# A decoder layer's expert lookup for three token tiles: row gathers replaced by two streamed tables and a gate matrix

## The chip, the cores and the metric

One of the eight cores of a Trainium2 chip runs the whole program. The metric is the device time of one execution in microseconds (us). All numbers are float32.

## The reference, cut to what matters

One layer over 512 prompt tokens (tiles 0 to 3 of 128 tokens) and 32 sample tokens (tile 4). First a mixing layer (input projection, gated MLP on chunks, windowed attention, output projection), then the expert layer below, then a final RMSNorm. The change is in the expert layer alone.

```
q = (xb @ w_q).reshape(TOK_BLK, PEER_HEADS, 2, DK_HALF)
s = jnp.einsum('thcd,hcnd->thcn', q, sub_keys).astype(jnp.float32)
s1, i1 = lax.top_k(s[:, :, 0], TOPK)
s2, i2 = lax.top_k(s[:, :, 1], TOPK)
...
eid = jnp.take_along_axis(cid, pos, axis=-1)
g = jax.nn.softmax(top_s, axis=-1).astype(xb.dtype)
hid = jax.nn.gelu(jnp.einsum('thkd,td->thk', u_tab[eid], xb), approximate=False)
return jnp.einsum('thk,thkd->td', g * hid, v_tab[eid])
```

With 8 heads and TOPK = 16 each token picks 128 of 16,384 experts. An expert is a row of 1,024 numbers in the table U and one in the table V (each table 67 MB). Its number is i1 * 128 + i2 of its two picks.

## The kernel before

Tensors lie with tokens or features on the 128 partitions. Each engine has its own instruction list and waits on semaphores; the order in each list is written out by hand. The stages in the order of TensorE's list:

- Tile 0 goes through projection, attention, output projection and its queries first. Its routing (the top-k chain on VectorE, `route(k)` for head k, cut into links that are dealt out between other work by `go_on`) gives expert numbers, and GpSimd begins to gather rows of U for it (`gather_u`).
- Tiles 1 to 4: projection (`project`), attention (`attend`), while VectorE takes the 128 dot products of tile 0 (`dots_to`).
- Output projection of tiles 1 to 4 (`project_out`), RMSNorm, `turn_xn` (the normalised tokens are transposed into `featT`), queries (`half_queries`, 416 columns each) and `key_scores`. Between these stand the V rows of tile 0: `gather_v` brings the 128 experts of one token as 128 rows (524 KB), and `weigh` multiplies them on TensorE with that token's weights. `weigh_first(4)` does four tokens, each in its own 32 columns of the array. The V ring has VR = 12 buffers.
- Tiles 1 to 3, then tile 4: the slot loop. Slot j of a tile is the j-th expert of each of its 128 tokens. `gather_both` brings 128 rows of U and V side by side (1.05 MB) into one of XR = 6 buffers; VectorE takes the dot product (`dot`); ScalarE makes gelu, times the gate, and a diagonal matrix of it (`weigh_slot`); TensorE multiplies that diagonal with the V rows and adds up in PSUM (`add_slot`, two matmuls of 512 columns). 20 slots of tile 1 are added by VectorE (`add_rows`). There are 3 x 128 slots for tiles 1 to 3 and 32 for tile 4, whose 32 tokens are spread over four groups of partitions. Routing of later tiles is dealt out between slots, and the last five of the eight query jobs (`JOBS`) stand between slots of tile 1.
- Each tile ends with `square_y`, `finish_y` and a store.

Of the kernel before, what the change touches and what calls it, by code (L numbers as in the profile page):

```python
# [10 lines left out]
AX = mybir.AxisListType  # L11
# [3 lines left out]
P = 128  # L15
# [32 lines left out]
NKEYS = 128  # L48
TOPK = 16
SLOTS = HEADS * TOPK  # L50
UR, VR, XR = 6, 12, 6
DG = 4
# [5 lines left out]
STEPS = [HEADS] * (NT - 1) + [HEADS // GROUPS]  # L58
FIRST = [sum(STEPS[:t]) for t in range(NT)]
NSTEP = sum(STEPS)  # L60

# [3 lines left out]
ROUTE_STEP = {g: [g + 2] for g in range(8, 24)} | {g: [2 * g - 22, 2 * g - 21] for g in range(24, 31)}  # L65
TOPS_ATT, EID_SAMPLE = 15, 5

JOBS_AHEAD = 3


def build(nc, x_p, x_s, k_cache, v_cache, gains, gain_cols, w_in, ln_gb, w_sT, b_sT, w_out, w_q, keysT, uv_tab,
# [3 lines left out]
    with ctx:  # L75
# [14 lines left out]
        def cut(area, a, *dims):  # L90
# [4 lines left out]
            if len(dims) == 3:  # L95
# [27 lines left out]
        x_ring = ([cut(area_r, s * 2 * D, 2 * D) for s in range(XR // 2)]  # L123
                  + [cut(area_r, 2 * PAIRS * TOK + s * 2 * D, 2 * D) for s in range(XR // 2)])
# [30 lines left out]
        y_junk = cut(area_v, NT * D, D)  # L155
# [17 lines left out]
        diag = [cut(area_c, s * P, P) for s in range(DG)]  # L173
# [3 lines left out]
        den = cut(area_v, (NT + 1) * D, NSTEP)  # L177
# [12 lines left out]
        tops = tops_all[:].rearrange("p (h k) -> p h k", h=HEADS)  # L190
# [28 lines left out]
        def wide(i, n):  # L219
            return bank[i].rearrange("p a b -> p (a b)")[:, 0:n]  # L220

        acc = bank[0]
        x_cur = wide(1, D)

# [31 lines left out]
        x_free, hid_ready, bent_ready, col_ready, diag_ready = (sem("x_free"), sem("hid_ready"), sem("bent_ready"),  # L256
                                                                sem("col_ready"), sem("diag_ready"))
        head_exped, head_gated, summed_den = sem("head_exped"), sem("head_gated"), sem("summed_den")
        eye_ready, numbered = sem("eye_ready"), sem("numbered")
        x_added, rest_added = sem("x_added"), sem("rest_added")  # L260
# [3 lines left out]
        samp_gates = sem("samp_gates")  # L264
# [78 lines left out]
        U_OF = [SLOTS] * (NT - 1) + [SLOTS // GROUPS]  # L343
        U_END = [sum(U_OF[:t + 1]) for t in range(NT)]
        V_OF = [n for _, n in TILES]

        X_END = [U_END[t] - U_END[0] for t in range(NT)]


        def x_slot(i):  # L350
            return (i + 1) % XR


        BY_DVE = [h * TOPK + j for h in range(HEADS - JOBS_AHEAD) for j in (4, 5, 9, 10)]

        def by_pe(i):
            return i - sum(d < i for d in BY_DVE)

        def tile_of(i):
            return next(t for t in range(NT) if i < U_END[t])  # L360


        N_ITER = NG - NG0 + 3
# [24 lines left out]
        def job_part(j):  # L388
            i, p = HEADS + JOBS_AHEAD + j // TOPK, {3: 0, 8: 1, 13: 2}.get(j % TOPK)
            return (i, p) if p is not None and i < len(JOBS) else None  # L390

# [14 lines left out]
        def sum_of(t):  # L406
            n = TILES[t][1]
            return x_tile[t][0:n, :] if t < SAMP else acc[0:n].rearrange("p a b -> p (a b)")
# [11 lines left out]
        def _(sp):  # L420
# [94 lines left out]
            sp.wait_ge(g_turned, NT)  # L515
            sp.wait_ge(roped, len(QK))
# [19 lines left out]
            for t in range(1, NT):  # L536
                load_x(t)
            for i in range(HEADS + 3, len(JOBS)):
                sp.wait_ge(q_done[1], i - 2)
                load_wq(wq_ring[(i - HEADS) % 3], JOBS[i][0], wq_again[(i - HEADS) % 3])  # L540
            sp.wait_ge(xn_ready, NT)
            sp.dma_start(gain[:], gains[2:3, :].broadcast_to([P, D])).then_inc(gain_in, 16)
            for t, (a, n) in enumerate(TILES):
                sp.wait_ge(y_ready, t + 1)
                if t < SAMP:
                    sp.dma_start(y_p[a:a + n, :], x_tile[t][0:n, :]).then_inc(y_out, 16)
                else:
                    sp.dma_start(y_s, x_tile[t][0:n, :]).then_inc(y_out, 16)
            sp.wait_ge(y_out, 16 * NT)
# [4 lines left out]
        def _(pe):  # L554
# [229 lines left out]
            def project_out(t, c, tokens=0):  # L784
# [9 lines left out]
                for k in range(KD):  # L794
                    if k == KD // 2:
                        weigh_first(tokens)
# [1198 lines left out]
```

## Time and profile before

| what | value |
|---|---|
| median of 3 executions | 1687.59 us (1683.56 to 1921.37) |
| profiled execution, first to last instruction (span) | 1709.3 us |
| mean granted TensorE clock | 0.956 of 2.4 GHz |
| TensorE busy | 1404.9 us (82%) |
| VectorE / ScalarE / GpSimd busy | 1085.5 / 634.5 / 652.7 us |
| moved by DMA | 664.81 MB, 389 GB/s |

The profiled execution is another one than the three timed ones. Its span is all that is recorded of its time, and it is 21.7 us above their median. PE is TensorE, PEld its weight loads, DVE VectorE, ACT ScalarE, POOL GpSimd, SP the engine that issues most loads. A float32 matmul stands in the trace as two records, each with a weight load.

### The profile page before, as it was taken

How to read it: one execution, taken by the hardware profiler on the slowest of the kernel's cores; microseconds unless marked ns; L12 is line 12 of the kernel's file. 1: busy time of each engine (PE TensorE's matmuls, PEld its weight loads, DVE VectorE, ACT ScalarE, POOL GpSimd, SP SyncE). 2: the span in 40 equal slices, each digit the busy share in tenths (PEclk: the TensorE clock that was granted, in tenths of full speed). 3: DMA queues.
4: the chain of work that ended last, by engine and by line, in shares of the span. 5: the costliest groups of instructions: out<-in, count | busy, mean ns of one | idle time of the engine just before them, and what ended most of it. 6: DMA issues, size and time to landing. Idle time of an engine off the chain costs nothing.

```text
span 1709.3 us, 17753 instructions
## 1 busy us (share of the span) xinstructions
PE 1404.9 (82%) x5164; PEld 622.7 (36%) x5164; DVE 1085.5 (64%) x2884; ACT 634.5 (37%) x1889; POOL 652.7 (38%) x703
## 2 busy tenths in 40 slices
PE   8999996768997978888878887777777777777786
PEld 5585663435333434334423232222223222222211
DVE  2459978868000046777766766666668888888654
ACT  2421113445211024344444454444445444444443
POOL 3034333322565653333333333333333333333332
PEclk9999996888998989999999999999999999999999
DMA  9798889999999999999999999999999999999997
GB/s 344 292 357 313 318 318 364 398 411 385 358 362 338 386 375 399 413 409 417 410 423 421 406 416 422 421 421 403 407 422 396 414 422 420 405 419 413 409 406 324
DMA packets 112144, 664.81 MB, mean 389 GB/s; under 512 B 13072, under 2 KB 14336, under 8 KB 52400
## 3 DMA queue, kind: packets, MB, share of 16 engines
q0 software_dynamic: 97824, 571.75, 83.4%
q1 hardware_dynamic: 14224, 91.93, 13.8%
q8 instruction: 42, 0.69, 0.2%
q14 instruction: 54, 0.44, 0.1%
HBM read 658.03 MB, written 5.60 MB: 388 GB/s over the span
## 4 chain that ended last, share of the span: by engine, by line
DMA 37%; PE 37%; issue 8%; ACT 7%; DVE 6%; another core or an unknown queue 3%; POOL 0%; ACTq 0%; SPq 0%; DVEq 0%; POOLq 0%
DMA area_r<-in_uv_tab,eid 36%; PE bank L907 11%; PE bank L627 9%; PE bank L851 4%; PE bank L896 4%; ACT area_c L1003 3%; PE bank L798 2%; DVE area_r L1703 2%; PE bank L558 1%; PE bank L871 1%; ACT L1253 1%; DVE area_x L1711 1%; DMA area_w<-in_w_in 1%; PE bank L767 1%
## 5 line engine op out<-in xcount | busy, mean ns | idle before, releaser
L907 PE MATMUL bank<-area_r,area_c 128*128 128x512 f32 (+1 forms) x1584 | 778.8, 624 | 213.8 <-ACT area_c L1003 212.8
L1873 POOL DMA_INDIRECT area_r<-in_uv_tab,eid x544 | 515.7, 948 | 944.0 <-PE bank L907 590.0
L1703 DVE CUSTOM_DVE_ANT_0 area_r<-area_r,bank 128x1024 f32<-128x1024 f32 x416 | 506.3, 1218 | 288.0 <-DMA area_r<-in_uv_tab,eid 287.3
L907 PEld LDWEIGHTS bank<-area_r,area_c 128*128 128x128 f32 (+1 forms) x1584 | 273.3, 188 | 713.0 <-issue 712.6
L1253 ACT ACTIVATE area_c<-hid 128x1 f32<-128x1 f32 x416 | 84.2, 202 | 538.8 <-DVE hid L1703 538.3
L1694 DVE CUSTOM_DVE_ANT_0 area_r<-area_r,bank 128x1024 f32<-128x1024 f32 x128 | 152.9, 1212 | 25.5 <-DMA area_r<-in_uv_tab,eid 22.7
L627 PE MATMUL bank<-area_w,area_t 128*128 128x384 f32 (+1 forms) x448 | 157.6, 509 | 4.1 <-DMA area_w<-in_w_in 3.5
L1003 ACT ACTIVATE area_c<-ident,area_c 128x128 f32<-128x128 f32 x364 | 146.1, 401 | 34.9 <-ACT area_c L1003 1.1
L1873 POOL DMA_INDIRECT area_r<-in_uv_tab,eidT x128 | 121.4, 948 | 82.0 <-issue 29.3
L1003 ACT ACTIVATE area_x<-bank 128x384 f32<-128x384 f32 (+8 forms) x123 | 49.9, 423 | 212.4 <-remote 59.4
L851 PE MATMUL bank<-area_t,area_w 128*128 128x416 f32 (+1 forms) x448 | 118.8, 418 | 6.1 <-issue 5.2
L1003 ACT ACTIVATE area_c<-gate,area_c 128x1 f32<-128x1 f32 x384 | 113.0, 294 | 13.9
L627 PEld LDWEIGHTS bank<-area_w,area_t 128*128 128x128 f32 x448 | 84.4, 192 | 68.0 <-issue 18.3
L851 PEld LDWEIGHTS bank<-area_t,area_w 128*128 128x128 f32 x448 | 70.4, 192 | 55.4 <-issue 54.1
L1397 DVE RECIPROCAL small<-small 128x1 f32<-128x1 f32 (+1 forms) x9 | 1.4, 158 | 113.3 <-issue 58.3
L896 PE MATMUL bank<-area_r,area_c 128*32 128x512 f32 x384 | 71.7, 633 | 0.9 <-issue 0.9
L1547 DVE MAX8 rt<-area_w 128x8 f32<-128x128 f32 (+1 forms) x80 | 19.3, 281 | 72.6 <-issue 52.0
L896 PE MATMUL bank<-area_r,area_v 128*32 128x512 f32 x128 | 64.4, 629 | 0.0
L798 PE MATMUL bank<-area_w,area_t 128*128 128x512 f32 x96 | 46.5, 631 | 1.7 <-issue 0.9
L1003 ACT ACTIVATE area_t<-bank 64x8 f32<-64x8 f32 (+5 forms) x111 | 28.6, 265 | 51.5 <-PE bank L558 28.3
L1487 DVE CUSTOM_DVE_ANT_0 area_x<-bank,area_c 128x256 f32<-128x256 f32 (+4 forms) x52 | 26.0, 535 | 23.9 <-PE bank L665 11.5
L1088 ACT ACTIVATE area_x<-area_x,att 128x256 f32<-128x256 f32 (+3 forms) x44 | 28.7, 653 | 31.2 <-DVE att L1487 19.1
(200 smaller groups left out, 1202.6 us busy)
## 6 DMA issues: line engine op xcount, KB each, us to landing
area_w<-in_w_in SPq DMA_DIRECT2D x12, 1536.0 KB, 11.1
area_w<-in_k_cache SPq DMA_DIRECT2D x8, 1920.0 KB
area_w<-in_w_q SPq DMA_DIRECT2D x14, 1024.0 KB, 6.8
area_r<-in_uv_tab,eid POOLq DMA_INDIRECT x544
area_w<-in_w_out SPq DMA_DIRECT2D x4, 2048.0 KB, 11.6
area_w<-in_v_cache SPq DMA_DIRECT2D x4, 1920.0 KB
area_v<-in_v_cache SPq DMA_DIRECT2D x4, 1152.0 KB
area_x<-in_x_p SPq DMA_DIRECT2D x6, 512.0 KB
```

Source lines behind the costliest of these rows:

```text
L627: mm = pe.matmul(out_half(u)[0:n, 0:w], featT[:, k, a:a + n], w_now[:, k, 0:w], start=(k == 0), stop=(k == KD - 1))
L798: mm = pe.matmul(ps[0:n, :], featT[:, k, a:a + n], w(k, c * 512, (c + 1) * 512), start=(k == 0), stop=False)
L851: mm = pe.matmul(half(4 + c)[:, 0:n], w[:, k, c * P:(c + 1) * P], featT[:, k, a:a + n], start=(k == 0), stop=(k == KD - 1))
L896: mm = pe.matmul(acc[CG * g:CG * g + CG, e, :], wd[g][:, c * CG:c * CG + CG], v_ring[s][:, e * 512:(e + 1) * 512], start=False, stop=False ...
L907: mm = pe.matmul(acc[0:n, c, :], diag[by_pe(i) % DG][:, 0:n], x_ring[s][:, D + c * 512:D + (c + 1) * 512], start=(i == 0), stop=False, ski ...
L1003: return nc.scalar.activation(out, src, ACT.Copy, scale=scale)
L1088: nc.scalar.activation(score_of(u)[0:r, 0:n], score_of(u)[0:r, 0:n], ACT.Exp, bias=st[0:r, 0:1], scale=-1.0, accum_out=st[0:r, 2:3]).then_ ...
L1253: nc.scalar.activation(bent[:, j:j + 1], hid[t % 2][:, j:j + 1], ACT.Gelu).then_inc(bent_ready, 1)
L1487: return vec.tensor_tensor_reduce(out=out, in0=scores, in1=counts, scale=-1.0, scalar=3e38, op0=ALU.add, op1=ALU.min, accum_out=least)
L1694: vec.tensor_tensor_reduce(out=u_ring[s], in0=u_ring[s], in1=x_cur, scale=1.0, scalar=0.0, op0=ALU.mult, op1=ALU.add, accum_out=hid[0][:, ...
L1703: vec.tensor_tensor_reduce(out=u, in0=u, in1=x_cur, scale=1.0, scalar=0.0, op0=ALU.mult, op1=ALU.add, accum_out=hid[t % 2][:, j:j + 1]).th ...
L1873: nc.gpsimd.indirect_dma_start(out=ring[s], out_offset=None, in_=table, in_offset=bass.IndirectOffsetOnAxis(ap=where, axis=0)).then_inc(la ...
```

## The change

For tiles 1 to 3 (384 tokens) nothing is gathered any more. In a first pass over 128 blocks of 128 experts, `hidden(b)` multiplies U block b with all 384 tokens (8 matmuls of 384 columns); ScalarE takes gelu (`gelu_block`) and the result goes to a scratch tensor in DRAM, 4 blocks a store. Beside it a matrix of gates is built: for each token, a one-hot of its 128 first picks times the gate (VectorE, `make_firsts`) and a one-hot of its second picks (GpSimd, `make_seconds`) are multiplied on TensorE into a 128 x 128 block (`build_weights`, four tokens in each of 96 steps, from block 17 on); ScalarE copies it out (`read_built`) and stores 32 tokens at a time (2.1 MB, one buffer). In a second pass over 128 blocks, gates and hidden values are loaded back, multiplied on VectorE (`weigh_block`), and `add_block` multiplies them with the V block (6 matmuls of 512 columns) into PSUM, one bank pair a tile. All eight query jobs stand ahead of the first pass. The V rows of tile 0 stand, four tokens each, behind the projections, five of the query jobs and 16 of the blocks (`ROWS_AT`), with VR = 8 buffers. The 32 slots of tile 4 keep their gathers, with XR = 2 buffers, in the second pass; VectorE adds them up, and `sum_samples` brings them to PSUM at block 122.

```diff
 GROUPS = P // NSAMP
...
+ND = len(DENSE) * P
+NU, NV, NA = 4, 4, 3
+HQ, HLOADS = 4, 3
+TB, WQN = 32, 8
+BUILT = 4
+NBUILD = ND // BUILT
+PER_TILE = P // BUILT
+PER_BATCH = TB // BUILT
 
...
+ROWS_QUERY = 5
+ROWS_AT = range(4, 95, 6)
+SUM_FIRST_AT = 97
+SAMPLE_FROM, SAMPLE_STEP = 20, 3
+SAMPLE_SUM_AT = 122
+Y_ORDER = (0, SAMP) + tuple(DENSE)
...
+            def load_u(b):
+                sp.dma_start(u_blk[b % NU], u_blocks[b]).then_inc(u_in[b % NU], 16)
+
+            def load_v(b):
+                sp.dma_start(v_blk[b % NV], uv_tab[b * P:(b + 1) * P, D:2 * D]).then_inc(v_in[b % NV], 16)
+
+            def load_weights(m):
+                src = w_scratch[:, :, m * WQN * TB:(m + 1) * WQN * TB].rearrange("t p f -> p t f")
+                sp.dma_start(w_load[m % 2].rearrange("p t b k -> p t (b k)"), src).then_inc(w_load_sem[m % 2], 16)
+
+            def load_hidden(n):
+                sp.wait_ge(h_stored[n % 2], 16 * (n // 2 + 1))
+                sp.dma_start(h_in[n % HLOADS].rearrange("p q k -> p (q k)"), h_scratch[n]).then_inc(h_in_sem[n % HLOADS], 16)
+
...
             sp.wait_ge(xn_ready, NT)
             sp.dma_start(gain[:], gains[2:3, :].broadcast_to([P, D])).then_inc(gain_in, 16)
-            for t, (a, n) in enumerate(TILES):
-                sp.wait_ge(y_ready, t + 1)
+            for b in range(NU, NBLK):
+                sp.wait_ge(h_done, b - NU + 1)
+                load_u(b)
+            sp.wait_ge(route_link, (DENSE[1] + 1) * HEADS * LINKS)
...
+            sp.wait_ge(v_free, VR + V_FIRST)
+            for n in range(HLOADS):
+                load_hidden(n)
+            sp.wait_ge(w_stored, 16 * (ND // TB))
+            load_weights(0)
+            sp.wait_ge(h_done, NBLK)
+            load_weights(1)
+            for b in range(NV, NBLK):
+                sp.wait_ge(v_used, b - NV + 1)
+                load_v(b)
+                n = (b - 1) // HQ + 2
+                if b % HQ == 1 and n < NBLK // HQ:
+                    sp.wait_ge(a_ready, HQ * (n - HLOADS + 1))
+                    load_hidden(n)
+                m = (b - 1) // WQN + 1
+                if b % WQN == 1 and 2 <= m < NBLK // WQN:
+                    sp.wait_ge(a_ready, WQN * (m - 1))
+                    load_weights(m)
+
...
-            def add_slot(t, j):
-                i = X_END[t - 1] + j
-                s, n = x_slot(i), TILES[t][1]
-                pe.wait_ge(x_landed[s], 16 * (i // XR + 1))
-                pe.wait_ge(diag_ready, by_pe(i) + 1)
...
+            def hidden(b):
+                pe.wait_ge(u_in[b % NU], 16 * (b // NU + 1))
+                if b >= 2:
+                    pe.wait_ge(gelued, b - 1)
+                for k in range(KD):
+                    mm = pe.matmul(half(4 + b % 2)[:, 0:ND], u_blk[b % NU][:, k * P:(k + 1) * P], featT[:, k, P:P + ND],
+                                   start=(k == 0), stop=(k == KD - 1))
+                mm.then_inc(h_done, 1)
+
...
+            def build_weights(w):
+                pe.wait_ge(firsts_ready, w + 1)
+                pe.wait_ge(seconds_ready, w + 1)
+                out = build_half(build_at["weights", w])
+                for q in range(BUILT):
+                    mm = pe.matmul(out[:, q * P:(q + 1) * P], hot_second[w % 2][:, q, :], hot_first[w % 2][:, q, :],
+                                   start=True, stop=True)
+                mm.then_inc(built, 1)
+
+            def add_block(b):
+                pe.wait_ge(v_in[b % NV], 16 * (b // NV + 1))
+                pe.wait_ge(a_ready, b + 1)
+                for t in DENSE:
+                    for c in range(2):
+                        mm = pe.matmul(sums[t][:, c, :], a_blk[b % NA][:, (t - 1) * P:t * P], v_blk[b % NV][:, c * 512:(c + 1) * 512],
+                                       start=False, stop=(b == NBLK - 1), skip_group_check=True)
+                    if b == NBLK - 1:
+                        mm.then_inc(tile_summed, 1)
+                if b < NBLK - 1:
+                    mm.then_inc(v_used, 1)
+
...
+                if i > HEADS:
+                    key_scores(i - 1)
+                half_queries(i, 1)
+                if i < HEADS + ROWS_QUERY:
+                    weigh_first(4)
+            key_scores(len(JOBS) - 1)
+            for c in range(2):
+                pe.wait_ge(q_copied[c], len(JOBS))
+            pe.wait_ge(s_ready, len(SCORED))
+            pe.wait_ge(u_free, UR + SLOTS)
+            for b in range(NBLK):
+                hidden(b)
+                if b in ROWS_AT:
+                    weigh_first(4)
+                for t in DENSE:
+                    if b == TURN_IDX[t]:
+                        turn_picked(t)
+                if 0 <= b - BUILD_FROM < NBUILD:
+                    build_weights(b - BUILD_FROM)
+            pe.wait_ge(acc_read, 1)
+            pe.wait_ge(build_read, len(build_at))
+            for t in DENSE:
+                start_sum(t)
...
-            def weigh_slot(t, j):
...
+            def gelu_block(b):
+                n = b // HQ
+                if b % HQ == 0 and n >= 2:
+                    act.wait_ge(h_stored[n % 2], 16 * (n // 2))
+                act.wait_ge(h_done, b + 1)
+                nc.scalar.activation(h_out[n % 2][:, b % HQ, :], half(4 + b % 2)[:, 0:ND], ACT.Gelu).then_inc(gelued, 1)
+
+            def store_hidden(n):
+                act.wait_ge(gelued, HQ * (n + 1))
+                nc.scalar.dma_start(h_scratch[n], h_out[n % 2].rearrange("p q k -> p (q k)")).then_inc(h_stored[n % 2], 16)
+
...
+            def read_built(w):
+                if w % PER_BATCH == 0 and w > 0:
+                    act.wait_ge(w_stored, 16 * (w // PER_BATCH))
+                act.wait_ge(built, w + 1)
+                r, k = build_at["weights", w], w % PER_BATCH * BUILT
+                copy(w_out_stage[:, :, k:k + BUILT],
+                     half(BUILD_HALF[r % len(BUILD_HALF)]).rearrange("p (q i) -> p i q", q=BUILT)).then_inc(build_read, 1)
+
+            def store_weights(m):
+                act.wait_ge(build_read, build_at["weights", (m + 1) * PER_BATCH - 1] + 1)
+                nc.scalar.dma_start(w_scratch[m], w_out_stage.rearrange("p i k -> p (i k)")).then_inc(w_stored, 16)
+
...
-            def dot(t, j):
-                i = X_END[t - 1] + j
-                s = x_slot(i)
-                dve.wait_ge(x_landed[s], 16 * (i // XR + 1))
...
-            def add_rows(i):
-                s, k, x = x_slot(i), BY_DVE.index(i), x_tile[1]
-                dve.wait_ge(col_ready, i + 1)
-                if k >= 1:
...
+            def make_firsts(w):
+                t, k, s = DENSE[w // PER_TILE], w % PER_TILE * BUILT, w % 2
+                first, gates = picked_T[t % 2][:, 0, :], picked_T[t % 2][:, 2, :]
+                if k == 0:
+                    dve.wait_ge(build_read, build_at["picked", t] + 1)
+                if w == 0:
+                    dve.wait_ge(numbers_in, 16)
+                if w >= 2:
+                    dve.wait_ge(built, w - 1)
+                for q in range(BUILT):
+                    ins = vec.tensor_scalar(hot_first[s][:, q, :], numbers, first[:, k + q:k + q + 1], gates[:, k + q:k + q + 1],
+                                            ALU.is_equal, ALU.mult)
+                ins.then_inc(firsts_ready, 1)
+
+            def weigh_block(b):
+                if b % WQN == 0:
+                    dve.wait_ge(w_load_sem[b // WQN % 2], 16 * (b // WQN // 2 + 1))
+                if b % HQ == 0:
+                    dve.wait_ge(h_in_sem[b // HQ % HLOADS], 16 * (b // HQ // HLOADS + 1))
+                if b >= NA:
+                    dve.wait_ge(v_used, b - NA + 1)
+                out, hid_in = [x.rearrange("p (t k) -> p t k", k=TB) for x in (a_blk[b % NA], h_in[b // HQ % HLOADS][:, b % HQ, :])]
+                vec.tensor_tensor(out, w_load[b // WQN % 2][:, :, b % WQN, :], hid_in, ALU.mult).then_inc(a_ready, 1)
 
             def weights():
                 dve.wait_ge(gelu_done, 1)
                 vec.tensor_tensor(hid[0], hid[0], gate[:], ALU.mult).then_inc(w_ready, 1)
 
...
-            def gather_both(t, j):
-                i = X_END[t - 1] + j
-                if j % TOPK == 0:
-                    pool.wait_ge(eid_ready, U_END[t - 1] // TOPK + j // TOPK + 1)
...
+            def make_seconds(w):
+                t, k, s = DENSE[w // PER_TILE], w % PER_TILE * BUILT, w % 2
+                if k == 0:
+                    pool.wait_ge(build_read, build_at["picked", t] + 1)
+                if w == 0:
+                    pool.wait_ge(numbers_in, 16)
+                if w >= 2:
+                    pool.wait_ge(built, w - 1)
+                for q in range(BUILT):
+                    ins = nc.gpsimd.tensor_scalar(hot_second[s][:, q, :], numbers, picked_T[t % 2][:, 1, k + q:k + q + 1], None,
+                                                  ALU.is_equal)
+                ins.then_inc(seconds_ready, 1)
+
+            used = [V_FIRST - 4 * sum(a > b for a in ROWS_AT) for b in range(NBLK)]
+            made = 0
+            for b in range(BUILD_FROM + NBUILD - 2):
+                ready = min(used[b] + VR, V_FIRST)
+                for j in range(made, ready):
+                    gather_v(j)
+                made = ready
+                if b >= BUILD_FROM - 2:
+                    make_seconds(b - BUILD_FROM + 2)
+            for j in range(SAMPLE_SLOTS):
+                gather_both(j)
 
 
 def counts_log(dist, reach):
```

## Rows read from the trace of the kernel before

**Rows 1.** The page: engines' busy time and share of the span.

```profile
PE 1404.9 (82%) x5164; PEld 622.7 (36%) x5164; DVE 1085.5 (64%) x2884; ACT 634.5 (37%) x1889; POOL 652.7 (38%) x703
```

**Rows 2.** Windows: stretch, its length, busy time of engines, clock, DMA share, GB/s.

```profile
130.00:263.00 133.00, 132.03 (x720) 80.26 (x718) 118.47 (x330) 21.18 (x61) 57.10 (x60) 1.00 0.89 320
263.00:450.00 187.00, 139.86 (x1138) 78.06 (x1140) 127.20 (x383) 86.49 (x284) 61.29 (x64) 0.83 0.99 390
450.00:500.00 50.00, 50.00 (x224) 18.02 (x220) 2.90 (x4) 7.65 (x13) 31.60 (x34) 1.00 0.94 345
500.00:560.00 60.00, 48.09 (x309) 20.36 (x302) 4.01 (x5) 8.14 (x19) 37.77 (x40) 0.86 0.95 341
...
640.00:1630.00 990.00, 792.89 (x1717) 304.00 (x1717) 722.31 (x1847) 428.92 (x1277) 363.37 (x385) 0.97 1.01 413
```

**Rows 3.** The page: the chain that ended last, by line.

```profile
DMA area_r<-in_uv_tab,eid 36%; PE bank L907 11%; PE bank L627 9%; PE bank L851 4%; PE bank L896 4%; ACT area_c L1003 3%; PE bank L798 2%; DVE area_r L1703 2%; PE bank L558 1%; PE bank L871 1%; ACT L1253 1%; DVE area_x L1711 1%; DMA area_w<-in_w_in 1%; PE bank L767 1%
```

**Rows 4.** Timeline of TensorE in the slot loop: start, length, idle before.

```profile
639.70 9.83 PE L907 MATMUL bank<-area_r,area_c 128*128 128x512 f32 x16 [4.96 <-ACT area_c L1003]
649.36 5.75 PE L851 MATMUL bank<-area_t,area_w 128*128 128x416 f32 x16
654.95 3.87 PE L907 MATMUL bank<-area_r,area_c 128*128 128x512 f32 x8
...
1005.40 1.96 PE L907 MATMUL bank<-area_r,area_c 128*128 128x512 f32 x4 [0.51 <-ACT area_c L1003]
1007.89 1.96 PE L907 MATMUL bank<-area_r,area_c 128*128 128x512 f32 x4 [0.54 <-ACT area_c L1003]
...
1627.12 12.16 PE L907 MATMUL bank<-area_r,area_c 128*32 128x512 f32 x24 [1.38 <-ACT area_c L1003]
```

**Rows 5.** Timeline of TensorE: matmuls of 128, then of 384 columns.

```profile
96.39 3.74 PE L851 MATMUL bank<-area_t,area_w 128*128 128x128 f32 x32
99.96 0.61 PE L871 MATMUL bank<-area_r,area_x 128*128 128x128 f32 x4
...
146.94 15.75 PE L627 MATMUL bank<-area_w,area_t 128*128 128x384 f32 x48
162.61 2.12 PE L624 MATMUL bank<-area_w,area_t 128*32 128x128 f32 x48
```

**Rows 6.** Chain of waits from 445 us: start, length, what.

```profile
445.12 3.70 PE bank L798 x8
...
454.32 0.86 PE bank L806 x2
455.18 1.87 PE bank L896 x16
```

**Rows 7.** Timeline of TensorE: last transposes and first query.

```profile
545.96 0.68 PE L558 MATMUL bank<-ident,area_v 32*128 32x32 f32 x8
552.32 4.75 PE L851 MATMUL bank<-area_t,area_w 128*128 128x416 f32 x8 [3.81 <-issue]
558.88 3.06 PE L851 MATMUL bank<-area_t,area_w 128*128 128x416 f32 x8
```

**Rows 8.** Groups of VectorE and GpSimd by form: busy, mean ns, idle before.

```profile
L1506 DVE TENSOR_SCALAR area_r<-area_r,att 128x128 f32<-128x128 f32 x12 | 3.4, 287 | 0.4
L1873 POOL DMA_INDIRECT area_r<-in_uv_tab,eidT x128 | 121.4, 948 | 82.0 <-issue 29.3 <-PE bank L896 26.6 <-remote 16.3
```

**Rows 9.** Timeline of VectorE: first and last operation of one head's routing.

```profile
624.07 0.49 DVE L1547 MAX8 rt<-area_w 128x8 f32<-128x128 f32 x2 [16.26 <-ACT area_w L1003]
...
633.66 0.18 DVE L1609 SCALAR_TENSOR_TENSOR eid<-rt 128x16 uint32<-128x16 f32 x1 [0.15 <-DVE rt L1604]
```

**Rows 10.** Groups of ScalarE by form.

```profile
L1003 ACT ACTIVATE area_x<-bank 128x384 f32<-128x384 f32 x24 | 11.4, 488 | 56.2 <-PE bank L627 47.1 <-issue 7.2 <-PE bank L719 1.8
L1003 ACT ACTIVATE area_x<-bank 128x512 f32<-128x512 f32 x18 | 10.5, 598 | 60.6 <-issue 19.8 <-PE bank L806 16.5 <-remote 15.7
```

**Rows 11.** The page: DMA issues, KB each, median us to landing.

```profile
area_w<-in_w_in SPq DMA_DIRECT2D x12, 1536.0 KB, 11.1
...
area_w<-in_w_out SPq DMA_DIRECT2D x4, 2048.0 KB, 11.6
...
area_w<-in_x_p SPq DMA_DIRECT2D x1, 512.0 KB, 3.7
```

**Rows 12.** Timeline of all engines behind the last matmul.

```profile
1704.00 1.01 ACT L1282 ACTIVATE area_v<-bank 32x1024 f32<-32x1024 f32 x1 [0.54 <-PE bank L907]
...
1705.72 1.27 DVE L1724 SCALAR_TENSOR_TENSOR area_x<-bank,small,gain 32x1024 f32<-32x1024 f32 x1
1707.02 0.33 SPq L548 DMA_DIRECT2D out_y_s<-area_x  x1
```

More of the change, by code:

```diff
@@ L57 @@
 LINKS = 12
-STEPS = [HEADS] * (NT - 1) + [HEADS // GROUPS]
-FIRST = [sum(STEPS[:t]) for t in range(NT)]
-NSTEP = sum(STEPS)
+NBLK = N_EXPERTS // P
+DENSE = range(1, NT - 1)
+ND = len(DENSE) * P
[6 more added lines that the diff above has]
+PER_BATCH = TB // BUILT
 DOTS_FIRST, DOTS_PROJ = 12, 75
@@ L189, in build @@
         tops_all = sb("tops", SLOTS)
[L190 removed]
+        tops = [(tops_other if t in (2, SAMP) else tops_all[:]).rearrange("p (h k) -> p h k", h=HEADS) for t in range(NT)]
         rt = sb("rt", 8 * TOPK)
@@ L548, in _ @@
                     sp.dma_start(y_s, x_tile[t][0:n, :]).then_inc(y_out, 16)
+            for i in range(NT):
+                store_y(i)
             sp.wait_ge(y_out, 16 * NT)
@@ L833, in turn_xn, with half_queries @@
                     mm.then_inc(xn_turned, 1)
-            def queries(i, tokens=0):
-                for c in range(2):
-                    half_queries(i, c, tokens)
-            def half_queries(i, c, tokens=0):
+            def half_queries(i, c):
                 h = JOBS[i][0]
@@ new lines, in build_half, with turn_picked @@
+            def build_half(r):
+                if r >= len(BUILD_HALF):
+                    pe.wait_ge(build_read, r - len(BUILD_HALF) + 1)
+                return half(BUILD_HALF[r % len(BUILD_HALF)])
+            def turn_picked(t):
+                pe.wait_ge(tile_gated, t)
+                out = build_half(build_at["picked", t])
+                for i, src in enumerate((picked[t % 2][:, 0, :], picked[t % 2][:, 1, :], gate[:])):
+                    mm = turn(out[:, i * P:(i + 1) * P], src, P)
+                mm.then_inc(idx_turned, 1)
@@ L1847, in _ @@
-            finish_y(SAMP)
+            dve.wait_ge(v_out, 16 * (NT + 1))
+            for h in range(HEADS):
+                go_on(route(HEADS * DENSE[0] + h))
+            links = {t: routings(range(HEADS * t, HEADS * (t + 1))) for t in range(DENSE[1], NT)}
+            go_on(links[2], 4)
+            finish_gates(DENSE[0])
+            go_on(links[2], 6)
+            for w in range(NBUILD):
+                t = DENSE[w // PER_TILE]
+                k = w % PER_TILE
+                if k == PER_TILE - 2 and t < DENSE[-1]:
+                    go_on(links[t + 1])
+                    finish_gates(t + 1)
+                make_firsts(w)
+                go_on(links[t + 1], 4 if t < DENSE[-1] else 2)
@@ new lines, in _ @@
+            go_on(links[SAMP])
+            set_x_samp()
+            sample_indices()
+            for b in range(NBLK):
+                weigh_block(b)
+                if b == 2:
+                    finish_gates(SAMP)
+                if b == 8:
+                    finish_y(0)
+                j, k = divmod(b - SAMPLE_FROM, SAMPLE_STEP)
+                if 0 <= j < SAMPLE_SLOTS:
+                    if k == 0:
+                        sample_dot(j)
+                    if k == 2:
+                        sample_add(j)
@@ L1849, in _ @@
+            for i in range(1, NT):
+                finish_y(i)
         @block.gpsimd
```

414 lines of the change are left out of this document (192 added, 222 removed).

## The prediction

> **What bounds the kernel now.** I read the page's busy times first: TensorE 82% of 1709.3 us, the others 64% and less [rows 1]. That alone would say "TensorE-bound". The chain of waits says otherwise: 36% of it are the gathers of expert rows and only 11% the slot loop's own matmuls, L907 [rows 3]. The windows explain it: in the slot loop, 640 to 1630 us, DMA is busy all the time at 413 GB/s [rows 2]. The timeline shows it slot by slot: 1.96 us of matmuls, half a microsecond idle, the next slot 2.48 us after the last [rows 4]. From 639.70 to 1627.12 us the 384 slots of tiles 1 to 3 take 987 us, 2.57 each, and one slot's 1.05 MB at 413 GB/s takes 2.54. So the loop is paced by gathers, with TensorE close behind: two limits some 20 to 25% apart. What the change does to the time is read from how much work it gives TensorE once the gathers are gone.
>
> **The price of a matmul.** Busy time overlaps and can't be used; I take the distance between starts. 384 columns: 48 records, which are 24 matmuls, in 162.61 - 146.94 = 15.67 us, 0.653 us each [rows 5]. 416 columns: 8 matmuls in 5.59 us, 0.699 each [rows 4]. 512 columns: 8 records in 3.70 us with the end, and 2 in 0.86 us without it, so 0.86 each [rows 6]. 128 columns: 16 matmuls in 3.57 us, 0.223 each [rows 5]. All four are 1.68 to 1.74 ns a column: the time goes with the columns, whatever the weights, at a clock of 1.00 [rows 2].
>
> **The change, part by part,** against the span of 1709.3 us.
>
> *Up to 445 us* nothing changes. VR = 8 in place of 12 touches only gathers after that.
>
> *Output projection to first query* (445.12 to 552.32 now [rows 6, 7]). The gathers of tile 0 pace it: two sets of four rows a half projection. After the change each half projection carries one set. The five full ones take 8 x 0.86 + 0.95 + 1.88 = 9.7 us each [rows 6], 49 us; the short tile 4, about 5 us (an estimate from its 32-column shapes); four sets of transposes 4; six more sets 11; and the norm of tile 4 ahead of the first query 6.4, as now [rows 7]. That is 75 us. Twenty-four tokens' rows (12.6 MB, 37 us at the 345 GB/s of this stretch [rows 2]) are wanted in the last 25 us with eight in the ring, so 0 to 15 us of stall; I take 3. First query at 523 us.
>
> *Queries.* All eight jobs now stand here: 16 halves x 5.6 us = 90 [rows 4]; key scores 8 x 8 matmuls x 0.223 = 14, with ScalarE's copies between about 21; five sets of rows 9. Together 120, and 3 for the last copies: 646 us. That is close to where the slot loop starts now (639.70), which had done three jobs and all 128 rows by then. The cover of the other five jobs, idle TensorE beside gathers, is gone, and they count in full.
>
> *First pass.* 128 x 8 matmuls of 384 columns x 0.653 = 669 us. 96 building steps of 4 x 0.223 + 0.1 for the change-over = 96. The remaining 16 sets of rows x 1.88 = 30 [rows 6]. Transposes of picks and block starts 7. Sum 802: ends at 1448.
>
> *Second pass.* Starting the three sums 5; 128 x 6 matmuls of 512 columns x 0.857 = 658; block starts 6; the samples' sum 4. Sum 673: ends at 2121.
>
> *Tail.* From the last matmul: 1.8 us on ScalarE, 1.6 on VectorE, 0.3 to issue [rows 12], and the store of 512 KB, taken as the 3.7 us of a load of that size [rows 11]. 7 us: a span of 2128.
>
> *What is taken away.* 396 slots on TensorE, 792 matmuls x 0.857 = 679 us of its work, against 669 + 96 + 658 = 1423 of new work. The slot loop and tile 4 took 1709 - 640 = 1069 us, the new part takes 1482. Bytes fall from 436 MB gathered in the loop to 67 for U, 67 for V, 101 for both scratch tensors out and back and 34 for tile 4, 269 MB in 1475 us: about 180 GB/s beside rows of tile 0, under half of the 413 that the loop reaches. The gain in bytes buys nothing, since TensorE has no room to be let free.
>
> *What lies beside it.* A block of the first pass takes 5.2 us, 6.2 with a building step, 6.5 with its share of rows. ScalarE: gelu of 384 columns and a copy of 512, 0.49 and 0.60 by the nearest rows [rows 10], perhaps double for the strided copy: 2 us, hidden. VectorE: four one-hots at 0.287 [rows 8] and four of a head's twelve routing links, 9.8 us a head [rows 9], make 1.15 + 3.3 = 4.4 us of 6.4, hidden, with three quarters used. GpSimd: four one-hots, and 4 gathers of 0.95 in six blocks. No row shows arithmetic on GpSimd. Low end 0.287 as on VectorE [rows 8], high end twice a gather, 1.9 us: 1.8 to 8.2 us a step against 6.4. I take the value near 0.5, because the shape is VectorE's, and nothing is lost; the high end costs 96 x 1.8 = 173 us. The store of 2.1 MB of gates has one buffer: `read_built` waits for it and stands ahead of the next gelu in ScalarE's list, and TensorE can go on for two blocks, about 11.5 us. Loads of 1.5 and 2 MB landed in 11.1 and 11.6 us at a nearly full DMA [rows 11]; at half load it should be 7 to 10. Nothing, or up to 11 x 4 = 44 us. In the second pass VectorE has one product (0.5 to 0.8 us) and 0.9 us of sample work a block of 5.2, and loads run two to four blocks ahead: nothing.
>
> The Trainium skill speaks against the split of the one-hots: in "SBUF — State Buffer", section "Who interferes with whom", a tensor_scalar on VectorE can take the port pair it shares with GpSimd for the whole instruction, and the other then fully blocks. By it GpSimd would wait up to four VectorE one-hots a step. No row here has arithmetic on both, so the trace neither bears it out nor refutes it. The page "GPSIMD Engine Reference", section "Engine selection", has one-input operations on GpSimd at roughly line rate; by that the sum stays as it is.
>
> **Rivals.**
>
> *GpSimd late in building.* The port or a slow one-hot makes a step longer than 6.4 us. At 1.9 us a one-hot a step takes 8.2 us: 2128 + 173 = 2301; anything from 2180 up counts here. For it: no row prices it, gathers queue between. Against: 128 elements is a small shape, two buffers give a step of slack.
>
> *The gate store holds ScalarE, and so TensorE.* 15 us a store would give 11 x 3.5 = 39 us: 2167. For it: one buffer and loads of 11 us. Against: DMA at under half load.
>
> *TensorE falls to half clock.* It does so after idle stretches (0.83 to 0.86 around attention and before the queries; the first query took 4.75 for 8 records, later ones 3.06 [rows 7]; clocks in [rows 2]). With no idle time in either pass there is no reason to; each percent of the two passes at 1.2 GHz costs 14 us.
>
> *The other side: not slower.* The 0.653 and 0.86 us would have to be paces set by something else, loads or VectorE's dots, and TensorE's own rate be faster. To come out at 1709, new matmuls must cost 0.70 of these, 1.17 ns a column; at half price the span is about 1420. Against: the same 1.7 ns a column at four widths, with DMA from 320 to 413 GB/s and VectorE nearly idle or nearly full [rows 2].
>
> **From these to numbers.** Forecast (TensorE-bound, 2080 to 2180): 0.76. GpSimd or VectorE late: 0.11. Gate store: 0.07, mostly inside the range. Clock: 0.04. Other side: 0.02. The timed median is 21.7 us under the profiled span. If that is a profile slowing the gathers, little of it is left in a kernel that TensorE paces; if it is a share, it is 27. I take 10 off: 2118 us. Low 2080: no stall and 0.64 us a matmul of 384 columns, with the whole offset taken off. High 2220: the store and part of the GpSimd case. Faster 0.02, same 0.01 (within 2%, about what a measurement here can tell from none), slower 0.97.
>
> **What would show it.** After the change: TensorE over 95% busy from some 520 us on, starts of hidden blocks 5.2 us apart before block 17 and 6.2 after, second-pass blocks 5.2 apart, DMA below 60% in both, the chain almost all TensorE on the two new matmul lines, and the passes meeting near 1450 us. A GpSimd or VectorE tile as what ended TensorE's idle time would show the first rival, ScalarE idle behind a DMA every eighth step the second. A matmul of 384 columns well under 0.64 us would make the whole forecast wrong.

## The result, and the profile after

2094.93 us median (2094.7 to 2097.7) against 1685.6 us before: ratio 1.2425 (95% interval 1.2399 to 1.2452), slower by 24%. The comparison leaves out the one disturbed execution of before, at 1921.37 us, which the median of 1685.6 includes. The forecast was 2118 us, with a range of 2080 to 2220. The profiled execution has a span of 2093.3 us and a time of 2095.12.

The page of the changed kernel, engines' busy time; it answers to [rows 1]:

```profile
PE 2026.8 (97%) x7945; PEld 1108.6 (53%) x7945; DVE 821.6 (39%) x2574; ACT 340.6 (16%) x860; POOL 530.1 (25%) x703
```

TensorE went from 82% to 97% of a longer span, VectorE from 64% to 39%, ScalarE from 37% to 16%. The chain of waits says the same; in [rows 3] its first entry was the gathers, with 36%:

```profile
PE bank L993 32%; PE bank L963 31%; PE bank L914 6%; PE bank L697 6%; PE bank L984 4%; DMA area_r<-in_uv_tab,eid 3%; PE bank L953 3%; PE bank L866 2%; PE bank L628 1%; PE bank L931 1%; PE bank L837 1%; DMA area_w<-in_w_in 1%; DMA area_x<-in_x_p 1%; DMA w_scratch<-area_w 1%; PE bank L789 1%
```

L963 are the matmuls of the first pass, L993 those of the second, L984 the building steps. The windows of both passes: busy time equals the length, the clock is at its upper level, DMA is little over half busy, and VectorE, ScalarE and GpSimd are all under half (the columns are those of [rows 2], TensorE's weight loads being the second busy number).

```profile
637.00:1418.80 781.80, 780.65 (x3081) 482.25 (x3082) 308.00 (x1204) 129.49 (x241) 295.44 (x442) 1.00 0.55 195
1424.00:2087.00 663.00, 663.00 (x1545) 292.25 (x1543) 148.20 (x227) 23.46 (x79) 28.10 (x30) 1.00 0.63 217
```

The timeline of TensorE gives the price of a block and of a step, by the distances between starts:

```profile
637.20 26.04 PE L963 MATMUL bank<-area_t,area_r 128*128 128x384 f32 x80 [0.62 <-issue]
...
1000.61 5.33 PE L963 MATMUL bank<-area_t,area_r 128*128 128x384 f32 x16
1005.77 1.05 PE L984 MATMUL bank<-area_r 128*128 128x128 f32 x8
1006.66 5.33 PE L963 MATMUL bank<-area_t,area_r 128*128 128x384 f32 x16
...
1418.83 5.31 PE L945 MATMUL bank<-area_x,ident 128*128 128x512 f32 x12
1423.98 6.60 PE L993 MATMUL bank<-area_w 128*128 128x512 f32 x15
```

A block takes 1005.77 - 1000.61 = 5.16 us (0.645 a matmul), a building step 0.89, and nothing stands between them. In the whole first pass TensorE waited 1.5 us, 0.9 of it for ScalarE. The slot loop of [rows 4] had half a microsecond of idle time in each slot; here that room is gone, and the new work on TensorE is about twice that of the slots it replaces.

### The profile page after: what moved, and what is told of

Same layout as the page of the kernel before. It is cut to its first block, busy times and chain, and to the rows that moved or that the text cites. A ratio compares the mean times of both kernels' runs of the same rounds, so it can differ in the third digit from the quotient of the medians.

```text
span 2093.3 us, 21893 instructions
## 1 busy us (share of the span) xinstructions
PE 2026.8 (97%) x7945; PEld 1108.6 (53%) x7945; DVE 821.6 (39%) x2574; ACT 340.6 (16%) x860; POOL 530.1 (25%) x703
## 2 busy tenths in 40 slices
DMA packets 129642, 497.37 MB, mean 238 GB/s; under 512 B 12512, under 2 KB 38480, under 8 KB 117504
## 4 chain that ended last, share of the span: by engine, by line
PE 90%; DMA 6%; DVE 2%; issue 2%; ACT 1%; POOL 0%; SPq 0%; DVEq 0%; ACTq 0%
PE bank L993 32%; PE bank L963 31%; PE bank L914 6%; PE bank L697 6%; PE bank L984 4%; DMA area_r<-in_uv_tab,eid 3%; PE bank L953 3%; PE bank L866 2%; PE bank L628 1%; PE bank L931 1%; PE bank L837 1%; DMA area_w<-in_w_in 1%; DMA area_x<-in_x_p 1%; DMA w_scratch<-area_w 1%; PE bank L789 1%
## 5 line engine op out<-in xcount | busy, mean ns | idle before, releaser
L963 PE MATMUL bank<-area_t,area_r 128*128 128x384 f32 x2048 | 677.7, 486 | 1.6 <-ACT area_v L1355 0.9
L993 PE MATMUL bank<-area_w 128*128 128x512 f32 x1536 | 659.6, 592 | 0.0
L963 PEld LDWEIGHTS bank<-area_t,area_r 128*128 128x128 f32 x2048 | 381.4, 190 | 249.0 <-issue 4.5
L993 PEld LDWEIGHTS bank<-area_w 128*128 128x128 f32 x1536 | 291.8, 190 | 367.7 <-issue 367.7
L2054 POOL TENSOR_SCALAR area_r<-area_v,area_w 128x128 f32<-128x128 f32 x384 | 237.7, 633 | 269.7 <-PE bank L984 236.6
L2012 POOL DMA_INDIRECT area_r<-in_uv_tab,eid x144 | 137.5, 955 | 656.0 <-DVE area_c L1822 203.8
L1835 DVE TENSOR_SCALAR area_r<-area_v,area_w 128x128 f32<-128x128 f32 x384 | 112.0, 356 | 312.3 <-PE bank L984 286.3
L1804 DVE CUSTOM_DVE_ANT_0 area_r<-area_r,bank 128x1024 f32<-128x1024 f32 x128 | 153.1, 1212 | 32.1 <-DMA area_r<-in_uv_tab,eid 31.8
L984 PEld LDWEIGHTS bank<-area_r 128*128 128x128 f32 x768 | 99.6, 191 | 32.4 <-issue 10.9
L984 PE MATMUL bank<-area_r 128*128 128x128 f32 x768 | 102.6, 276 | 0.0
```

Of the source, the lines that this page charges most:

```text
L963: mm = pe.matmul(half(4 + b % 2)[:, 0:ND], u_blk[b % NU][:, k * P:(k + 1) * P], featT[:, k, P:P + ND], start=(k == 0), stop=(k == KD - 1))
L984: mm = pe.matmul(out[:, q * P:(q + 1) * P], hot_second[w % 2][:, q, :], hot_first[w % 2][:, q, :], start=True, stop=True)
L993: mm = pe.matmul(sums[t][:, c, :], a_blk[b % NA][:, (t - 1) * P:t * P], v_blk[b % NV][:, c * 512:(c + 1) * 512], start=False, stop=(b == N ...
L1804: vec.tensor_tensor_reduce(out=u_ring[s], in0=u_ring[s], in1=x_cur, scale=1.0, scalar=0.0, op0=ALU.mult, op1=ALU.add, accum_out=hid[0][:, ...
L1835: ins = vec.tensor_scalar(hot_first[s][:, q, :], numbers, first[:, k + q:k + q + 1], gates[:, k + q:k + q + 1], ALU.is_equal, ALU.mult)
L2012: nc.gpsimd.indirect_dma_start(out=ring[s], out_offset=None, in_=table, in_offset=bass.IndirectOffsetOnAxis(ap=where, axis=0)).then_inc(la ...
```

## Experiments

All spans and times are of single profiled executions, except where an interval stands.

**e1, half of the first pass's matmuls.**

```diff
-                for k in range(KD):
+                for k in range(KD // 2):
                     mm = pe.matmul(half(4 + b % 2)[:, 0:ND], u_blk[b % NU][:, k * P:(k + 1) * P], featT[:, k, P:P + ND],
-                                   start=(k == 0), stop=(k == KD - 1))
+                                   start=(k == 0), stop=(k == KD // 2 - 1))
```

> The changed kernel, but each block of the first pass is multiplied over features 0 to 511 only (4 matmuls of 384 columns in place of 8); the other half of the hidden values is left out. U is loaded as before. Theory, the first pass is TensorE's columns and nothing else: 512 matmuls x 0.645 us = 330 us less on TensorE, and the pass then meets the next engine. A building step would take TensorE 2.58 + 0.89 = 3.47 us, VectorE 1.1 + 3.3 = 4.4 us while four routing links are dealt out a step (64 steps), GpSimd 2.5 + 0.6 = 3.2 us. So the pass falls from 782 to about 490 us and the kernel by some 290 us, to 1805 us. Rival, gate stores or GpSimd already pace it: a store keeps ScalarE 11 us, against two blocks of slack that are now 7 us; that gives back 4 us x 11 and more, and the kernel falls by 250 us or less, with TensorE idle behind ScalarE or behind the one-hots of GpSimd.

1842.39 us: 252.7 less by the spans, where 290 were expected. TensorE's work, at the price of 0.645 us a matmul, fell by 330. What TensorE waited for from 630 to 1150 us (us in total, times, longest):

```profile
PE bank L963 <- ACT area_v L1355: 29.3, 10, 5.9
PE bank L984 <- issue: 5.9, 7, 2.8
PE bank L963 <- DMA area_r<-in_u_blocks: 4.4, 4, 1.7
PE bank L984 <- POOL area_r L2054: 1.8, 1, 1.8
PE bank L984 <- DVE area_r L1835: 1.0, 3, 0.4
```

The next thing met is ScalarE, held behind the gate store ten times for 3 us, as the rival said, and not VectorE's 4.4 us a step: undisturbed steps run at 3.47 us. The first pass took 511.9 us in place of 781.6, so 60 of the 330 us were not gained in it: some 42 are the waits above. The rest is TensorE itself, which did its work at a granted clock of 0.97 on the mean, its busy time falling by 311 us and not by 330. Another 13.5 us stand idle between the passes, for VectorE's first product. So the mechanism of the theory held (the time goes with the columns until another engine is met), and its size was 37 us off: the next engine was the rival's, and the clock was left out.

**e2, building matmuls twice.**

```diff
-                for q in range(BUILT):
+                for q in [*range(BUILT), *range(BUILT)]:
                     mm = pe.matmul(out[:, q * P:(q + 1) * P], hot_second[w % 2][:, q, :], hot_first[w % 2][:, q, :],
```

> The changed kernel, with each of the 384 building matmuls made twice (same operands, same result). Theory, TensorE is the limit and its work adds up: 384 x 0.223 us = 86 us more, 2181 us. Rival, TensorE waits for one-hots or for ScalarE in the building steps and has room there: well under 86 us more.

2174.27 us, 79.2 more by the spans (2172.5 - 2093.3). This run reached the first pass 3.4 us earlier (633.79 against 637.20 us), so the pass itself grew by 82.6 of the 86 us. There is no room in a building step.

**e3, one-hots of GpSimd twice.**

```diff
+                for q in range(BUILT):
+                    nc.gpsimd.tensor_scalar(area_x[:, (s * BUILT + q) * P:(s * BUILT + q + 1) * P], numbers,
+                                            picked_T[t % 2][:, 1, k + q:k + q + 1], None, ALU.is_equal)
                 for q in range(BUILT):
```

> The changed kernel, with each one-hot of GpSimd made twice (the second into a spare place): 384 more operations of 0.63 us. Theory, GpSimd is hidden: a step costs it 8 x 0.63 + 0.63 for gathers = 5.7 us of TensorE's 6.05 (6.4 with rows): 0 to 15 us more. Rival, GpSimd or the port that it shares with VectorE is at the edge already: 384 x 0.63 = 243 us of new work, of which 100 us or more shows.

2094.96 us: no change. The groups of GpSimd show both sets (busy, mean ns of one, idle before):

```profile
L2054 POOL TENSOR_SCALAR area_x<-area_v,area_w 128x128 f32<-128x128 f32 x384 | 235.9, 628 | 78.2 <-PE bank L984 50.6 <-ACT area_w L1111 27.1
L2057 POOL TENSOR_SCALAR area_r<-area_v,area_w 128x128 f32<-128x128 f32 x384 | 230.1, 614 | 0.0
```

230 us of new GpSimd work cost nothing: GpSimd's part of the building is hidden. Beside it VectorE's one-hots took 378 ns on the mean in place of 356. How little the two engines hold each other up in the changed kernel shows where both start together:

```profile
903.47 1.17 DVE L1835 TENSOR_SCALAR area_r<-area_v,area_w 128x128 f32<-128x128 f32 x4 [4.89 <-PE bank L984]
903.52 2.42 POOL L2054 TENSOR_SCALAR area_r<-area_v,area_w 128x128 f32<-128x128 f32 x4 [3.63 <-PE bank L984]
915.63 2.33 POOL L2054 TENSOR_SCALAR area_r<-area_v,area_w 128x128 f32<-128x128 f32 x4 [3.63 <-PE bank L984]
```

GpSimd's four take 2.42 us beside VectorE's four, and 2.33 two steps later, where VectorE starts only at 917.79 us. A wait for all four of VectorE's (1.17 us), which the prediction named as possible, is not there.

**e4, the kernel before with gathers of half the bytes.**

```diff
-                gather(x_ring, x_slot(i), uv_tab, eid[:, a:a + 1], x_landed)
+                gather(x_half, x_slot(i), single, eid[:, a:a + 1], x_landed)
```

(`x_half` is the first half of each buffer; dot, add_slot and add_rows read it.)

> The kernel before, where each of the 416 gathers of the slot loop brings one row of 4 KB an expert in place of U and V side by side; the dot product and the sum both take that one row, so the values are others, and V is left out. All instructions of TensorE, VectorE and ScalarE stay. Theory, the loop was paced by gathers (2.57 us a slot) with TensorE close behind: a gather now takes 1.27 us, TensorE needs 1.71 + some change-over, VectorE 1.3 + 0.75 of routing = 2.05 us a slot; so 2.05 us a slot and about 215 us less, 1470 us. Rival, the loop is paced by the chain of waits from dot over gelu to diagonal and not by bytes: no change beyond 50 us.

1479.6 us, 210 less than the kernel before in the same run (1689.71). The number of DMA packets is the same, 112144; the bytes fell from 664.81 to 446.71 MB. The slots of tiles 1 to 3 ran from 612.43 us to the first slot of tile 4 at 1416.83: 2.09 us each in place of 2.57. From 640 to 1410 us TensorE was busy for 700 of 770 us and VectorE for 674; which of the two limits a slot now was not separated. By the spans the gain is 231.5 us: 183 in these slots, 21 in tile 4, and 27 ahead of the loop, where the profiled execution of before was late (see below). The slots of tile 4, with no routing beside them, show TensorE's limit at its plainest:

```profile
612.43 8.80 PE L908 MATMUL bank<-area_r,area_c 128*128 128x512 f32 x16 [4.36 <-ACT area_c L1004]
...
1416.83 55.59 PE L908 MATMUL bank<-area_r,area_c 128*32 128x512 f32 x128 [1.05 <-ACT area_c L1004]
```

32 slots in 55.6 us, 1.74 each: that is TensorE alone. So before, the loop was paced by bytes, and with half of them gone the kernel gains 210 us before other engines pace it. This is about the gain that fewer bytes had to offer, and the change paid for it with twice the matmul work.

**e5, both passes in bfloat16.** The core of the edit; the buffers, scratch tensors and one-hots become bfloat16 views in the same way:

```diff
-                sp.dma_start(u_blk[b % NU], u_blocks[b]).then_inc(u_in[b % NU], 16)
+                nc.gpsimd.dma_start(u_blk[b % NU], u_blocks[b]).then_inc(u_in[b % NU], 16)
...
-                    mm = pe.matmul(half(4 + b % 2)[:, 0:ND], u_blk[b % NU][:, k * P:(k + 1) * P], featT[:, k, P:P + ND],
+                    mm = pe.matmul(half(4 + b % 2)[:, 0:ND], u_blk[b % NU][:, k * P:(k + 1) * P], featB[:, k, :],
...
+                    if t in DENSE:
+                        copy(featB[:, 4 * i:4 * i + 4, a - P:a - P + n], src)
```

> The changed kernel with the matmuls of both passes and the building steps in bfloat16: U and V are cast while GpSimd's DMA queue loads them, ScalarE writes tokens, gelu and gates in bfloat16, both scratch tensors are bfloat16 (half the bytes). Queries, top-k, tile 0 and tile 4 stay float32. Precision is changed, and nothing is left out. Theory, the loss is the price of a float32 column: 1.68 ns in place of 0.42, so TensorE needs 1.3 us a block in either pass, and the passes meet other limits. First pass: VectorE 32 heads x 9.8 us of routing + 384 x 0.3 = 430 us, of which about 80 lie in the queries: 350 to 420 us in place of 782. Second pass: V 67 MB, scratch 25 MB and samples 34 MB at 413 GB/s = 305 us, VectorE 0.56 + 0.9 us a block: 300 to 380 us in place of 663. Together 1330 to 1480 us: faster than both kernels. Rival, the passes are bound by the way through DRAM and by waits, and TensorE's share only hides them: 1700 us or more.

1437.09 us median, ratio to the kernel before 0.8512 (0.8475 to 0.8549): faster than both. The windows of its two passes:

```profile
647.00:1095.50 448.50, 289.06 (x1673) 143.73 (x1674) 311.72 (x1209) 127.13 (x242) 374.21 (x570) 0.83 0.85 199
1100.90:1437.10 336.20, 214.69 (x760) 76.76 (x774) 120.88 (x225) 21.27 (x73) 103.24 (x154) 0.87 1.02 266
```

The first pass took 448 us where I expected 350 to 420, and I had named the wrong engine: GpSimd (fifth busy number), and not VectorE (third), fills 374 of the 448.5 us, with one-hots, gathers and the loads that I had put on its queue, and its one-hots alone are 44% of the chain of waits in this stretch. The second pass lies inside its 300 to 380. What paces it is DMA: share 1.02 at 266 GB/s, and TensorE waited 115.5 us for V in it. TensorE idles in short stretches and its granted clock falls to 0.83 and 0.87 on the mean.

**e7, the same with each bfloat16 matmul made four times.** In each loop of the three kinds of matmul:

```diff
-                for k in range(KD):
+                for k in [*range(KD)] * 4:
```

> The bfloat16 version with every matmul of both passes and of the building steps made four times: hidden values and gates come out as before, the sums of the second pass are taken four times over, so tiles 1 to 3 get other values. Bytes, types, queues and all other engines are as in the bfloat16 version; TensorE streams as many columns as in float32 (a float32 matmul takes 1.68 ns a column, a bfloat16 one 0.42). Theory, the passes of the changed kernel are priced by columns times four and nothing else: 2095 us again, within 30. Rival, the bfloat16 version was fast because scratch bytes were halved or the loads were moved: it stays under 1700 us.

2101.57 us. (The sums of the second pass are taken four times over, so the values of tiles 1 to 3 are others.) Types, bytes, queues and scratch are those of e5, only TensorE's columns are back, and the time is back within 6.5 us of the changed kernel's. The timeline of TensorE has the old 5.2 us a block and 0.9 a step, now as 32 and 16 records:

```profile
1001.39 1.07 PE L981 MATMUL bank<-area_r 128*128 128x128 bf16 x16
1002.30 5.36 PE L960 MATMUL bank<-area_r 128*128 128x384 bf16 x32
1007.50 1.06 PE L981 MATMUL bank<-area_r 128*128 128x128 bf16 x16
```

A float32 matmul is priced like four bfloat16 ones over the same columns, and that price is the whole difference between 2095 and 1437 us.

**e6, the gate store twice.**

```diff
                 nc.scalar.dma_start(w_scratch[m], w_out_stage.rearrange("p i k -> p (i k)")).then_inc(w_stored, 16)
+                nc.scalar.dma_start(w_other[m], w_out_stage.rearrange("p i k -> p (i k)")).then_inc(w_stored, 16)
```

(All waits for the store count both.)

> The changed kernel, with each store of 32 tokens' gates made twice (the second to another scratch tensor), so that ScalarE waits for 4.2 MB in place of 2.1. One store holds it for 8.6 us on the mean, and TensorE lost 0.95 us to that once. Theory, there are two blocks of slack, about 12 us: with 17 us of waiting the 11 waits cost 5 us each, 50 us more. Rival, the store was never near TensorE: no change within 10 us.

2144.99 us, 50 more. In the changed kernel, then here, what ScalarE and TensorE waited for in the first pass:

```profile
ACT area_w L1111 <- DMA w_scratch<-area_w: 94.7, 11, 12.3
...
PE bank L963 <- ACT area_v L1355: 0.9, 1, 0.9
```

```profile
ACT area_w L1112 <- DMA w_other<-area_w: 162.0, 11, 19.4
...
PE bank L964 <- ACT area_v L1356: 32.9, 11, 8.1
```

ScalarE's wait rose from 8.6 us on the mean to 14.7, and TensorE paid with 11 idle stretches of 3 us on the mean. The other 17 us stand behind them. Here is the longest, on TensorE's timeline:

```profile
1075.57 1.05 PE L985 MATMUL bank<-area_r 128*128 128x128 f32 x8
1084.70 8.32 PE L964 MATMUL bank<-area_t,area_r 128*128 128x384 f32 x16 [8.08 <-ACT area_v L1356]
1092.86 1.05 PE L985 MATMUL bank<-area_r 128*128 128x128 f32 x8
1093.75 5.33 PE L964 MATMUL bank<-area_t,area_r 128*128 128x384 f32 x16
```

The block behind 8 us of idle takes 8.16 us, the next one 5.16. The window of that block shows why; TensorE is busy throughout, and its granted clock is 0.64 on the mean:

```profile
1084.70:1092.86 8.16, 8.16 (x16) 4.52 (x17) 0.00 (x0) 1.22 (x3) 0.00 (x0) 0.64 0.00 0
```

TensorE began the block at its lower clock. So a wait costs more than its length. The longest wait of the changed kernel, 12.3 us, is just over the two blocks of slack, and cost 0.9. The single buffer was at its edge, and hardly over it.

**e8 and e9, two steps further from e5.** e8 has seven V buffers (`NV = 7`, with the samples' gathers four blocks later in GpSimd's list, since V loads are issued three blocks earlier), e9 also moves one of four second one-hots to VectorE:

```diff
+                q = BUILT - 1
+                ins = vec.tensor_scalar(hot_second[s][:, q, :], numbers, picked_T[t % 2][:, 1, k + q:k + q + 1], None, ALU.is_equal)
                 ins.then_inc(firsts_ready, 1)
...
-                for q in range(BUILT):
+                for q in range(BUILT - 1):
                     ins = nc.gpsimd.tensor_scalar(hot_second[s][:, q, :], numbers, picked_T[t % 2][:, 1, k + q:k + q + 1], None,
```

> The bfloat16 version with seven buffers for V in place of four. TensorE waited 115 us for V in the second pass. Theory A, that is latency behind GpSimd's queue: three more blocks of lead take away 40 to 80 us. Theory B, the DMA engines are full (their busy share was 1.02 in this stretch at 260 GB/s): 0 to 15 us.

> As the version with seven V buffers, and one of the four second one-hots of each building step is made by VectorE. GpSimd was busy 301 of 364 us in the first pass and stands on 14% of the chain. Theory A, GpSimd paces the first pass: 96 x 0.62 = 60 us of its work goes, less what VectorE (248 of 364 us busy) becomes late: 30 to 55 us less than with seven buffers alone. Theory B, VectorE's routing or DMA paces it: no change.

e8: 1431.17 us, ratio 0.8488 (0.8438 to 0.8539), not to be told from e5. Its waits in the second pass:

```profile
PE bank L990 <- DVE area_w L1846: 105.1, 30, 11.2
...
PE bank L990 <- DMA area_w<-in_uv_tab: 6.6, 1, 6.6
```

The wait for V went from 115.5 to 6.6 us, and 105.1 us of waiting for VectorE's product came in its place. VectorE waited for loads in turn, of sample rows and of gates from scratch (1060 to 1428 us):

```profile
DVE area_w L1811 <- DMA area_w<-in_uv_tab,eid: 49.0, 12, 5.9
DVE area_w L1846 <- DMA area_r<-w_scratch: 48.1, 6, 13.8
DVE area_r L1811 <- DMA area_r<-in_uv_tab,eid: 47.4, 11, 5.5
...
DVE area_w L1846 <- DMA area_w<-w_scratch: 18.4, 3, 8.1
```

The DMA share in the second pass was 1.04 at 277 GB/s. That is theory B: the DMA engines are full, and more buffers only change who is late. What was not tried is a third buffer for the gate loads, which took 20.7 to 25.8 us to land here, and 7.6 to 8.2 with the same bytes over the longer passes of e7.

e9: 1414.04 us, ratio 0.838 (0.8343 to 0.8416), 17 us under e8 where 30 to 55 were expected. TensorE's waits before the building matmuls, in e8, then in e9:

```profile
PE bank L981 <- issue: 68.3, 31, 6.0
PE bank L981 <- DVE area_r L1834: 11.5, 8, 5.5
```

```profile
PE bank L981 <- DVE area_r L1837: 57.1, 32, 3.9
PE bank L981 <- issue: 19.3, 8, 4.3
```

The wait that the profile puts down to nothing fell by 49 us as GpSimd's work went, and the wait for VectorE's one-hots grew by 46: VectorE, busy for 250 of 364 us (636 to 1000 us) in e8 and for 272 in e9, became the late one, and most of the relief was given back. It is the fastest version here, 275 us under the median of before taken in that run (1688.67), at a lower precision in the expert sums of tiles 1 to 3. No run has the kernel before in bfloat16, so what the change itself is worth at that precision was not measured.

## Why the prediction was right

*Bound before: gathers, TensorE close behind.* Shown by e4: half the bytes give 210 us, and the next limit of a slot is 2.09 us, against the 2.05 worked out for it.

*The price by columns.* The step that carries the forecast. Measured 0.645 us for 384 columns (0.653 forecast); the second pass's 663 us agree with 0.857 for 512. e2 and e7 show it from both sides: added columns cost 82.6 of the 86 us that they should, and columns alone bring the 2095 us back.

*The sum, term by term.* First query at 516.8 us (523 forecast). Two errors meet here. The first is the sentence that nothing changes up to 445 us. Nothing changes in the work there, but the profiled execution of before was late. The first two half projections of the changed kernel, then of the kernel before:

```profile
421.22 9.17 PE L866 MATMUL bank<-area_w,area_t 128*128 128x512 f32 x16 [0.62 <-ACT area_t L1111]
...
436.44 7.03 PE L866 MATMUL bank<-area_w,area_t 128*128 128x512 f32 x16
```

```profile
432.12 9.52 PE L798 MATMUL bank<-area_w,area_t 128*128 128x512 f32 x16 [0.94 <-issue]
...
445.12 3.70 PE L798 MATMUL bank<-area_w,area_t 128*128 128x512 f32 x8 [0.78 <-ACT area_v L1003]
```

In all ten other kernels profiled, this first one starts between 412.5 and 429.2 us. So the sum began 8.7 us too late. From there to the first query it took 80.4 us, 2.4 more than the 78 of the sum. Queries to the first pass 120.4 us (123). First pass 781.6 (802): 8 us less from the blocks, 11 from the building steps, where I had added 0.1 us each for a change-over that does not exist. Starts 5.2 (5), second pass 663.2 (668), tail 6.1 (7). Nearly all errors went one way, 35 us of span together: the late start, the price of 384 columns, and small allowances for gaps that a full TensorE queue does not have.

*Offset between span and time.* I took 10 us off, for a profile that might slow the gathers. The changed kernel's execution has a span 1.8 us under its time, so these 12 us offset a part of the 35: 23 us remain, from 2118 to 2094.93. That is partly luck. The span of before, 1709.3 us, stands against times of 1678.55 to 1693.65 us in other executions than the disturbed one, so the profiled one was itself slow by some 20 us, but not in the slot loop, where I looked for it: in e4, with the same instructions up to there, the first query started at 528.97 us in place of 552.32. The changed kernel did not have the 8.7 us that were lost ahead of 445 us, and the 10 happened to be about that size. Why that execution was late is not settled.

*The range.* Its low end does not follow to the microsecond: no stall, 0.64 us a matmul and 27 us off give 2085, not 2080. The result lies inside either way.

*What lies beside it.* VectorE's one-hots took 356 ns (287 taken), GpSimd's 633 (500 taken, 287 to 1900 as bounds); both hidden, the second with a margin of 230 us (e3). The gate store: ScalarE waited 8.6 us for it on the mean (7 to 10 forecast for the store), hidden but for 0.9 us, and e6 and e1 place its edge at two blocks, as worked out.

*Rivals.* GpSimd late: fell with e3. Gate store: did not decide, but its mechanism is real. Clock: 1.00 in both passes. Not slower: fell with the first profile.

## What to carry to other kernels

Bytes saved are worth only the distance to the next engine: read that distance first (here 0.48 us of a 2.57 us slot), then price the work that the saving adds by the distance between starts of the same shape, not by busy time. Replacing a gather by a dense product multiplies matmul work, and in float32 that is four times as dear: this change loses 24% in float32, and with its own matmuls in bfloat16 the same scheme runs 15 to 16% under the float32 kernel before. A single buffer whose wait stands ahead of other work in an engine's list has a fixed slack; name it in blocks, since it shrinks as the blocks get faster.

## What the runs showed of the hardware

A small tensor_scalar of 128 x 128 takes 633 ns on GpSimd and 356 on VectorE (with two operations in one) while both make them, against 287 for one operation on VectorE in [rows 8]. Most of the difference on VectorE goes with the second operation: in e9, where both forms stand beside GpSimd's one-hots and write bfloat16, the one with one operation took 303 ns and the one with two 371. In the bfloat16 version, loading U and V with a cast cut the bytes moved from 497.37 to 379.66 MB together with the smaller scratch, yet the DMA engines were full at 266 GB/s, where the slot loop reached 413 with large rows [rows 2].
